# The last layer's modulation as running sums on VectorE, and finer waits at the ends of attentions, in the mixing output and before turned heads

## The reference

```python
mod = (jax.nn.silu(c) @ w_mod[l] + b_mod[l])[:, None, :]
mod_c = jax.nn.silu(c_ctx) @ w_mod[l] + b_mod[l]
sh1, sc1, ga1, sh2, sc2, ga2 = jnp.split(mod, 6, axis=-1)
csh1, csc1, cga1, csh2, csc2, cga2 = jnp.split(mod_c, 6, axis=-1)
h = modulate(rms_norm(x, g_pre_mix[l]), sh1, sc1)
```

## Time and profile before

| | us |
|---|---|
| median of 3 executions | 2728.67 |
| lowest and highest | 2728.22, 2731.36 |
| profiled execution, its own time | 2730.54 |
| span of its profile | 2728.8 |
| mean granted clock of TensorE | 0.987 |

### The profile page before, as it was taken

How to read it: one execution, slowest core, us unless ns; L and a number is a source line. 1 busy time by engine, 2 the same in 40 slices (tenths; PEclk the granted TensorE clock), 3 DMA queues, 4 the chain that set the end, 5 groups by cost and what they waited for, 6 DMA issues and landing times.

```text
span 2728.8 us, 40372 instructions
## 1 busy us (share of the span) xinstructions
PE 2613.9 (96%) x14676; PEld 2125.0 (78%) x14676; DVE 1668.7 (61%) x2518; ACT 1384.1 (51%) x2241; POOL 104.1 (4%) x112
## 2 busy tenths in 40 slices
PE   8999999998999999899999999999999899999998
PEld 7768888676888888778876777778777678667997
DVE  5665545756998999445555544653454457456776
ACT  5645435654777777433435453532333544455655
POOL 2000001000000000000000100100000110010000
PEclk9999999999999999999999999999999899999999
DMA  7439795445999998332331224453553244334464
GB/s 229 132 125 277 250 313 162 126 131 171 320 332 324 326 317 303 95 78 62 85 89 55 75 65 128 124 178 124 163 166 96 78 109 132 96 105 138 141 193 155
DMA packets 353481, 448.03 MB, mean 164 GB/s; under 512 B 19872, under 2 KB 198176, under 8 KB 353312
## 3 DMA queue, kind: packets, MB, share of 16 engines
q1 hardware_dynamic: 349792, 435.44, 50.9%
q0 software_dynamic: 3232, 9.97, 1.3%
q10 hardware_dynamic: 288, 0.36, 0.0%
HBM read 444.63 MB, written 1.08 MB: 163 GB/s over the span
## 4 chain that ended last, share of the span: by engine, by line
PE 85%; DVE 7%; ACT 4%; issue 3%; DMA 1%; DVEq 0%; POOL 0%; SPq 0%; ACTq 0%; POOLq 0%
PE ps L2512 21%; PE ps L2499 18%; PE ps L2560 17%; PE ps L2573 8%; PE ps L2564 4%; PE ps L2878 2%; PE ps L2889 2%; PE ps L2581 2%; PE ps L2768 2%; PE ps L2909 2%; PE ps L2453 2%; DVE w_lo L1632 1%; PE ps L2599 1%; ACT w_hi L1103 1%; PE ps L2871 1%
## 5 line engine op out<-in xcount | busy, mean ns | idle before, releaser
L1632 DVE TENSOR_TENSOR w_lo<-raw,w_hi 128x1024 fp32r<-128x1024 f32 (+1 forms) x578 | 686.2, 1198 | 531.4 <-ACT w_hi L1103 449.5
L1103 ACT ACTIVATE w_hi<-raw 128x1024 fp32r<-128x1024 f32 (+1 forms) x578 | 589.9, 1031 | 319.9 <-PE ps L2512 128.8
L2560 PE MATMUL ps<-w_hi,h_hi 128*128 128x512 f32 (+1 forms) x992 | 403.8, 409 | 12.8 <-DVE h_lo L2123 6.5
L2560 PE MATMUL ps<-w_hi,h_lo 128*128 128x512 f32 (+1 forms) x992 | 379.9, 385 | 0.0
L2499 PE MATMUL ps<-h_hi,w_hi 128*128 128x256 f32 (+1 forms) x1008 | 300.4, 323 | 0.0
L2573 PE MATMUL ps<-w_lo,h_hi 128*128 128x512 f32 (+1 forms) x992 | 298.2, 384 | 0.0
L2499 PE MATMUL ps<-h_lo,w_hi 128*128 128x256 f32 (+1 forms) x1008 | 296.0, 319 | 0.0
L2560 PEld LDWEIGHTS ps<-w_hi,h_hi 128*128 128x128 f32 x992 | 187.4, 189 | 71.2 <-issue 31.8
L2499 PEld LDWEIGHTS ps<-h_hi,w_hi 128*128 128x128 f32 x1008 | 191.6, 190 | 30.3 <-issue 16.1
L2573 PEld LDWEIGHTS ps<-w_lo,h_hi 128*128 128x128 f32 x992 | 183.3, 188 | 39.5
L2560 PEld LDWEIGHTS ps<-w_hi,h_lo 128*128 128x128 f32 x992 | 187.5, 189 | 29.5 <-issue 1.0
(11 more groups left out here) (317 smaller groups left out, 4153.9 us busy)
## 6 DMA issues: line engine op xcount, KB each, us to landing
raw<-in_w_in SPq DMA_DIRECT2D x196, 512.0 KB, 3.7
arena<-in_w_mod SPq DMA_DIRECT2D x96, 512.0 KB, 5.6
raw<-in_w_up SPq DMA_DIRECT2D x88, 512.0 KB, 4.3
raw<-in_w_gu_exp SPq DMA_DIRECT2D x64, 512.0 KB, 5.5
arena<-in_w_gu_exp SPq DMA_DIRECT2D x64, 512.0 KB, 4.9
arena<-in_w_gu_exp SPq DMA_DIRECT2D x64, 384.0 KB, 3.9
arena<-in_w_dn_exp SPq DMA_DIRECT2D x48, 512.0 KB, 6.3
raw<-in_w_gu_dense SPq DMA_DIRECT2D x44, 512.0 KB, 7.4
```

The lines of the kernel that those rows point to most:

```text
L1103: nc.scalar.activation(w_hi[:, half, 0:n], place[:, 0:n], ACT.Copy).then_inc(seg.sig.hi_ready, 1)
L1632: nc.vector.tensor_tensor(w_lo[:, half, 0:n], place[:, 0:n], w_hi[:, half, 0:n].bitcast(F32), ALU.subtract).then_inc(seg.sig.lo_ready, 1)
L2560: ins = mm(ps[:, 2 * h + p % 2, 0:width], x[:, k + c, p * P:(p + 1) * P], wh[:, c * width:(c + 1) * width], start=opens and c == 0 and x i ...
```

## The change

- **Modulation of layer 1.** `ffn_units` of the conv feed-forward gets no modulation units. A new class `SummedMods` plans 48 parts (six results of 1024 columns by 8 chunks of 128 rows). SyncE loads a part of 128x1024 into one of three places, VectorE multiplies it by a column of the conditioning vector (one scalar for each partition) and adds it to a running sum (`add_parts`); the two results that the context needs too have two sides and two sums. When a result's 8 parts are in, TensorE adds over the partitions and puts the row in its place with four matmuls by a column of ones (`spread_sums`), ScalarE copies the bank once an iteration, and `mod_cols` adds the bias to another arrangement.
- **Modulation of layer 0** stays on TensorE, with four units in each second block (0, 2, ... 10) of an iteration.
- **Ends of attentions.** `last_beside` moves the last step of the forgetting, grouped and neighbourhood attentions behind part 0 of unit 0 of the branch that reads them; each unit of a branch waits for the pairs that it reads; the remaining steps are spread over the same units as before.
- **Mixing output.** Each part waits for its own tile.
- **Turned heads.** In the first block `heads_ready` rises after the gains, and the attention's additions wait for a new `decay_ready`. In the second block's layer 0 the context's queries are turned first, after the gains, and the third job waits for the rest.

```diff
+MOD_ORDER, MOD_BOTH, MOD_GAP, ONE_AT, MOD_PACE = (2, 3, 4, 5, 0, 1), 2, 2, 16, (0.95, 0.65, 0.7)
...
+class SummedMods:
+    def __init__(self, weights, iters, n, ups, places, sums, one):
+        self.weights, self.places, self.sums, self.one = weights, places, sums, one
+        self.steps, self.loads, self.shut, self.last, self.ends = {}, {}, {}, {}, []
+        spent = 2.0
+        for u in range(len(MOD_ORDER) * DC):
+            if u == (len(MOD_ORDER) - 1) * DC:
+                spent += MOD_GAP
+            at = int(spent)
+            self.steps.setdefault((at // n, at % n), []).append(u)
+            self.loads.setdefault(at + 1, []).append(u)
+            spent += self.sides(u // DC) * MOD_PACE[0 if at < ups + 2 else 1 if at < n else 2]
+            if u % DC == DC - 1:
+                self.ends.append(at)
+        for r, at in enumerate(self.ends):
+            at = at if at < ups + 4 else max(at, n + 3)
+            self.shut.setdefault((at // n, at % n), []).append(r)
...
-                these = mods[len(mods) * b // FB:len(mods) * (b + 1) // FB]
+                these = [] if b % 2 else mods[2 * b:2 * b + 4]
...
+        def last_beside(step, seg):
+            step.steps -= 1
+            seg.ride.setdefault((0, 0), []).append((step, step.steps))
...
-            halves["first"], halves["all"] = second.at["turn"], count["turn"]
+            halves["first"], halves["all"], halves["each"] = second.at["turn"], count["turn"], tiles
...
-                                       add=[(row_of_b[:, 2 * pr + hh, :], decay_parts[:, 0:(t + 1) * P], None),
+                                       add=[(row_of_b[:, 2 * pr + hh, :], decay_parts[:, 0:(t + 1) * P], (decay_ready, l + 1)),
...
-            spread(fox, units_of(*gates_fx, *under))
+            beside_fox = units_of(*gates_fx, *under)
             under = [branch(a["w_o_fox"][l], dt, TT, y_fx, g_fx, gates_fx[dt], 1, y_pairs=count["pair"]) for dt in range(2)]
+            last_beside(fox, under[0])
+            spread(fox, beside_fox)
...
-            took(ml_ready=1, heads_ready=1)
+            took(ml_ready=1, heads_ready=nq // TT)
...
+            heads_step = turn_heads(heads_q[TT:] + [j for t in range(nn) for j in (heads_q[t:t + 1] if t < TT else []) + heads_k[t:t + 1]])
+            if nq > TT:
+                heads_step.later = nq - TT
...
+            last_beside(grouped, under[0])
+            paced_steps(grouped, *beside_grouped)
...
+            last_beside(near, under[0])
+            paced_steps(near, *beside_near)
...
-            seg = add_segment("ffn", ffn_units(a["w_up_2"][l], a["w_down_2"][l], a["w_mod_2"][l + 1] if more else None), D_FF // FE,
+            seg = add_segment("ffn", ffn_units(a["w_up_2"][l], a["w_down_2"][l]), D_FF // FE,
...
+            def load_parts(seg, it, j):
+                sm = seg.summed
+                for u in sm.loads.get(it * seg.n + j, ()):
+                    if u < 3:
+                        sp.wait_ge(split_done, seg.clear)
+                    else:
+                        sp.wait_ge(part_added, sm.added(u - 3))
+                    r, k = u // DC, u % DC
+                    sp.dma_start(sm.places[u % 3], sm.weights[k * P:(k + 1) * P, MOD_ORDER[r] * D:(MOD_ORDER[r] + 1) * D]).then_inc(parts_loaded[u % 3], 16)
...
+                        if seg.summed is not None and (it, j) in seg.summed.last:
+                            act.wait_ge(sum_spread, seg.summed.last[it, j])
+                            nc.scalar.activation(seg.mod_rows[it], ps[:, 2, 0:2 * P], ACT.Copy).then_inc(mod_saved, 1)
...
+            def add_parts(seg, it, j):
+                for u in sm.steps.get((it, j), ()):
+                    r, k = u // DC, u % DC
+                    dve.wait_ge(parts_loaded[u % 3], 16 * (u // 3 + 1))
+                    w = sm.places[u % 3]
+                    for s in range(sm.sides(r)):
+                        n = sm.sum_no(r, s)
+                        dst, by = sm.sums[n % 3], cond[:, k, COND + s:COND + s + 1]
+                        if k == 0:
+                            if n >= 3:
+                                dve.wait_ge(sum_spread, n - 2)
+                            ins = nc.vector.tensor_scalar(dst, w, by, None, ALU.mult)
+                        else:
+                            dve.wait_ge(part_added, sm.added(u - 1) - sm.sides(r) + s + 1)
+                            ins = nc.vector.scalar_tensor_tensor(dst, w, by, dst, ALU.mult, ALU.add)
+                        ins.then_inc(part_added, 1)
...
+                    if st.rows is not None or st.nq > TT and j == 7:
+                        dve.sem_inc(heads_ready, 1)
...
-                        .then_inc(heads_ready, 1)
+                        .then_inc(decay_ready, 1)
...
+            def spread_sums(seg, it, j):
+                for r in sm.shut.get((it, j), ()):
...
+                    for s in range(sm.sides(r)):
+                        pe.wait_ge(part_added, sm.added(r * DC + DC - 1))
+                        row = 2 * (r - sm.first[it]) + s
+                        for g in range(4):
+                            ins = mm(ps[32 * g:32 * g + 32, 2, 0:2 * P], sm.one[:, ONE_AT - row:ONE_AT - row + 32],
+                                     sm.sums[n % 3][:, g * 2 * P:(g + 1) * 2 * P],
...

+                        ins.then_inc(sum_spread, 1)
...
-                    pe.wait_ge(split_done, seg.turned["first" if k + m <= DC // 2 else "all"])
-                if opens and q == 0 and seg.y_pairs:
-                    pe.wait_ge(y_saved, seg.y_pairs)
+                    turned_by = seg.turned["first" if k + m <= DC // 2 else "all"]
+                    if "each" not in seg.turned:
+                        pe.wait_ge(split_done, turned_by)
+                if q == 0 and seg.y_pairs:
+                    pe.wait_ge(y_saved, seg.y_pairs - (BC - k - m) * seg.tiles)
...
+                    if "each" in seg.turned and q == 0:
+                        pe.wait_ge(split_done, turned_by - seg.turned["each"] + p + 1)
...
                 if i == 0:
                     banks_free(st)
+                    pe.wait_ge(heads_ready, st.at["heads_ready"] - (1 if st.later else 0))
+                if st.later and i == st.later:
                     pe.wait_ge(heads_ready, st.at["heads_ready"])
```

More of the change, by code:

```diff
@@ L208, in loaded, with sides, added, sum_no @@
         return 16 * ((self.unit0 - self.apart + it * self.splits + self.split_at[j]) // RAW)
+class SummedMods:
[15 more added lines that the diff above has]
+            self.shut.setdefault((at // n, at % n), []).append(r)
+        phases = [[r for g, rs in self.shut.items() for r in rs if g[0] == it] for it in range(iters)]
+        self.first = [min(p) for p in phases] + [len(MOD_ORDER)]
+        for it, p in enumerate(phases):
+            at = next(g for g, rs in self.shut.items() if max(p) in rs)
+            self.last[it, at[1] + AHEAD] = self.sum_no(max(p) + 1, 0)
+    def sides(self, r):
+        return 2 if MOD_ORDER[r] < MOD_BOTH else 1
+    def added(self, u):
+        return sum(self.sides(i // DC) for i in range(u + 1))
+    def sum_no(self, r, s):
+        return sum(self.sides(i) for i in range(r)) + s
 class Step:
@@ L362, in build @@
         mods_done = sem("mods_done")
+        parts_loaded = [sem(f"parts_loaded_{i}") for i in range(3)]
+        part_added = sem("part_added")
+        sum_spread = sem("sum_spread")
         split_hi_done = sem("split_hi_done")
@@ L393, in build @@
         heads_ready = sem("heads_ready")
+        decay_ready = sem("decay_ready")
         ml_ready = sem("ml_ready")
@@ L883, in second_layer @@
             mod_rows = (view(FREE + 6144, 2 * P), view(FREE + 6144 + 2 * P, 2 * P))
-            mod_places = [view(at, UNIT) for at in (0, UNIT, 2 * UNIT, 3 * UNIT, NQK_AT)]
             more = l + 1 < DEPTH
-            seg = add_segment("ffn", ffn_units(a["w_up_2"][l], a["w_down_2"][l], a["w_mod_2"][l + 1] if more else None), D_FF // FE,
-                              A=H, N=nq * P, tiles=nq, mod_rows=mod_rows if more else None, mod_places=mod_places,
+            seg = add_segment("ffn", ffn_units(a["w_up_2"][l], a["w_down_2"][l]), D_FF // FE,
+                              A=H, N=nq * P, tiles=nq, mod_rows=mod_rows if more else None,
                               evac="conv", tmp=view(FREE + 4096, 4, 2 * T), o=o, cw=col_second(l, "conv_w"),
@@ L890, in second_layer @@
             seg.tail = Step("tail", dict(count), rows=mod_rows if more else None, l=l + 1)
+            if more:
+                seg.summed = SummedMods(a["w_mod_2"][l + 1], seg.iters, seg.n, 2 * FB, [view(i * UNIT, UNIT) for i in range(3)],
+                                        [view(at, UNIT) for at in (3 * UNIT, NQK_AT, FREE + 6656)], view(FREE + 7680, ONE_AT + 32))
             seg.gains = gains(1, l, nq // TT, view(FREE + 4096, 2, D))
@@ L2455, in use_mod @@
                 ins.then_inc(mods_used, 1)
+            def spread_sums(seg, it, j):
+                sm = seg.summed
```

(15 more changed lines are left out.)

44 lines of the change are left out of this document (33 added, 11 removed).

## The result

| | before | after |
|---|---|---|
| median of 5 executions, us | 2730.2 | 2711.88 |
| lowest and highest, us | 2728.22, 2733.64 | 2704.53, 2713.27 |
| profiled execution, us (span) | 2730.54 (2728.8) | 2707.75 (2706.0) |
| ratio of after to before, 95% interval | | 0.9922, 0.9911 to 0.9933 |

The kernel is faster by 18 us by the medians (21 by the ratio), not by the 51 us of the forecast: 2712 us lies above the range of 2669 to 2693. Lines after the diff moved: L1103 is now L1175 (w_hi), L1632 L1707 (w_lo), L2560 L2696 and L2573 L2709 (paced matmuls), L2499 L2631 and L2512 L2644 (feed-forward), L2878 L3018 (scores), L2889 L3029 (transposes of the probabilities), L2909 L3049 (values), L2225 L2327 (VectorE's last operation on a probability tile), L2209 L2311 (its maximum).

What follows compares the result with a forecast made beforehand. TensorE, busy for 96% of the span, was taken to bound the kernel. Gains of 25.3 + 3.0 + 8.6 + 5.3 + 8.3 = 50.5 us gave 2679 us, forecast range 2672 to 2685, 8 in 10 from 2669 to 2693.

Steps and rivals of the forecast that it cites:

- conv modulation: Conv feed-forward of layer 0: modulation off TensorE saves 29.4 us, spreads cost 4.1, net 25.3 us.
- dense by fours: Dense feed-forward: modulation units by fours in every second block leave fewer groups and breaks, 3.0 us gained.
- turned heads: Transposes before attentions: 6.6 us of waits go, plus slow clock 1.5 and restarts 0.5; 8.6 us, 6.6 if clock falls elsewhere.
- mixing output: Output matmuls waiting by tile: 6.5 us of h_lo waits and seven restarts by 0.27 go, 8.3 us.
- attention ends: Six attentions' last step moved into the following branch: y_lo stall of 5.1 us goes but for about 0.2; 5.3 us net.
- new places of the other steps: Attentions: the other 18 steps lie evenly over their units; effect on probability waits taken as nothing, within 2 us.
- more than the sum: Rival, chance 0.08: the even spread also removes probability waits, up to 2.5 us per first-block attention; 2673 us.
- The finer waits only move: Rival, chance 0.20: stalls return at the branch's second unit or the next tile; half of 22 us kept, 2690 us.
- The cover on VectorE: Conv stage: 64 operations at 1.28 us, 82 us in all, fit under TensorE's work; costed at nothing.
- The rival's formula: Slower rival, chance 0.03: at x us per VectorE addition the conv stage overruns; gain lost at 2.8, 2738 us at 3.0.
- a lead of 14.5 us: Conv stage: w_lo is made when unit j-3 is done and needed two units and 16 matmuls later, 14.5 us.
- no starving: Rival, chance 0.08: dense stage starves if bursts fetch 300 GB/s instead of 332; gain of 3.0 us gone, 2683 us.

Runs made afterwards that it cites:

- experiment 4: Kernel before with only the turned heads' finer waits and the mixing output's wait by tile: 2716.51 us, ratio 0.9947.
- experiment 5: Also moved_step_alone: kernel before with only the attentions' moved last step and the branch's wait by units, other steps at before's places: 2726.12 us, ratio 0.9980.
- old_places: Changed kernel with the attention steps that stay in the spread put back at the units of the kernel before: 2687.47 us, ratio 0.9844.
- new_places_alone: Kernel before with only the attention steps but the last placed as in the changed kernel, the last kept in the last unit: 2761.68 us, ratio 1.0119.
- additions_3us: Changed kernel with remaining attention steps at before's places, plus two idle products behind each of 64 VectorE additions: 2731.58 us, ratio 1.0004.

## Why the prediction was wrong

| term | forecast, us | measured, us | from |
|---|---|---|---|
| conv modulation | 25.3 | 23.7 | same matmuls in the two traces |
| dense by fours | 3.0 | 2.8 | same |
| turned heads | 8.6 | 8.5 | same |
| mixing output | 8.3 | 6 | 14.5 of experiment 4, less 8.5; 5.8 by its trace |
| attention ends | 5.3 | 5.5 | experiment 5 |
| new places of the other steps | 0, within 2 | -24 | medians of after and old_places |

They sum to 22.5 us; the medians give 18 and the ratio 21 (by ratios the last row is -21). The start of the profiled execution was 2.2 us longer too. In old_places, whose code is that of the change there, it was 0.4 us longer, so I put it to no part of the change.

**The step that failed** is the sentence "The other 18 steps now lie evenly over their units; what the probability waits do from it I take as nothing, within 2 us either way". The number 18 held for four of the six attentions; in layer 0 of the second block it is 34. The cost came from the second block, where 15 steps over 8 units became 14 and 31 became 30. "Evenly" was the wrong thing to look at: evenness in time hardly changed, parity did. It could have been read before the run: the row of 15.6 us in 16 was TensorE's largest wait for probabilities, and the two quotients written out show odd starts from the fifth unit on. The rival "more than the sum" had the right term with the wrong sign. "The finer waits only move" gave 2690 for stalls that move to the branch's second unit or the next tile; experiment 5 shows none at the former, and experiment 4 only 0.02 us at the latter and 0.9 us one stage later.

**Conv modulation.** The removed 29.4 us were right. The spreads were mis-sized: a spread of one sum took 0.57 us and of two 1.00, where I took 0.36 and 0.57, because I counted float32 matmuls like those of rounded halves. With the breaks: 4 x 0.83 + 2 x 1.26 = 5.8 us instead of 4.1.

**The cover on VectorE** held, with more room than I gave it. Multiply-adds took 1.279 us, against the 1.28 taken, and the products 0.747 instead of 1.28. The Trainium skill (VectorE: DVE Perf Modes, on Mode 2x_2P) has a float32 operation on one tensor in SBUF use both read ports, at twice the rate of one with two tensors. The trace agrees in direction: 747 against 1279 ns is 1.7 times. The rival's formula, 45x - 65 less 10 us of lead, gives 15 us at 2.0 and 46.5 at 2.7. Measured were 2.3 and 44: right near the price at which the rival began, since with the gain of old_places (43 us) the run at 2.7 came out level with the kernel before, but 13 us too dear at 2.0. The prediction had itself worked out a lead of 14.5 us and took off only 10. Taking off 14.5 once gives 11 and 42; taking it off in each iteration gives 3 (8.2 and 17.5 us of overrun, the first covered, 3.0 of the second left) and 28. No single lead fits both runs, so how much the queue hides between the two prices is open.

**Turned heads.** The waits went as told, 6.6 us of them. The clock is luck in part: the window that had 0.74 has 1.00 after, but it has that also in new_places_alone (and in moved_step_alone), where TensorE stands for the same 2.0 us at the same place:

```profile
118.00:124.00 6.00, 3.96 (x22) 3.14 (x21) 3.35 (x6) 1.74 (x3) 0.00 (x0) 1.00 0.52 148
```

Both were 1.5 to 1.8 us ahead of the kernel before by 131 us without having touched the heads. So about 1.5 of the 8.5 us are a price that the profiled execution before paid and others did not; how often it is paid, single traces can't say. The prediction had left room for that ("6.6 if the clock falls elsewhere"). **Mixing output** lost its waits, 6.5 us, but the term also counted seven restarts by 0.27. Only the one with four tiles came off. The three stalls of 0.28 us gave back themselves and no more, and in the three outputs with two tiles the restart stayed, behind the wait of 0.02 us; with the 0.9 us lost before the dense stage that makes 5.8 us instead of 8.3. **Dense stage and DMA**: no starving at 340 GB/s.

## What to carry to other kernels

- When steps of a software pipeline are laid over units by an integer quotient, write the quotient out for both counts before calling a change of count free. Here which two steps shared a unit was worth 20 to 24 us, as much as all finer waits gained (20); keeping pairs together gained 10 more.
- A coarse wait may be removed and its stall be gone, yet the kernel gets slower by what was shuffled to make room for it. Change the wait and the placement in separate runs.
- VectorE work put under TensorE can be nearly free up to a point and then cost almost in full: here 44 us more of it cost 2, the next 44 cost 42.

## What the hardware showed that I had not expected

- A float32 matmul of 32 columns by 256 shows as two records, and a group of four takes 0.57 us, as long as eight with rounded operands.
- TensorE's clock in additions_3us: around stalls of 4.0 and 2.6 us the granted clock was 0.73 and 0.66 over 10 us (a mean of the two levels, 1.2 and 2.4 GHz), while a stretch with stalls of 0.22 and 1.05 us kept it at 1.00, and so did the one in which a stall of 3.3 us ended:

```profile
1780.00:1790.00 10.00, 8.72 (x38) 6.58 (x37) 8.97 (x11) 4.46 (x6) 0.00 (x0) 1.00 0.70 203
...
1890.00:1900.00 10.00, 8.09 (x36) 6.68 (x37) 9.86 (x11) 1.69 (x2) 0.00 (x0) 1.00 0.55 161
```

In the changed kernel two stalls of 1.74 us and the end of a third between 2360 and 2380 us left it at 1.00 as well, with TensorE busy for 15.7 of those 20 us:

```profile
2360.00:2380.00 20.00, 15.73 (x108) 10.88 (x109) 9.49 (x22) 9.89 (x21) 0.00 (x0) 1.00 0.26 79
```

The Trainium skill (TensorE: Matmul & The Clock Gate, on the HAM clock gate) has the clock fall to its default of half rate where activity is missing; the rows with falls here agree, each with a stall in it, but a stall's length does not tell the outcome: one of 3.3 us left the clock at 1.00, and at 2.0 us both are seen, at two places of one trace and at one place in two traces (0.74 before, 1.00 in new_places_alone).
